# Eight more adaLN modulation units on VectorE: a quad in the first MLP's last group, another from the end of the GLA scan

## The reference, cut to what matters

```python
def adaln(cond, w, b):
    m = jax.nn.silu(cond) @ w + b            # (1 or 2 rows, 2048) @ (2048, 12288), once a layer
    m = m.reshape(cond.shape[0], 6, 1, D_MODEL)
    return [m[:, j] for j in range(6)]

hp = modulate(xp, norm_g[l, 0], sh1p, sc1p)  # rmsnorm(x, g) * (1 + scale) + shift
...
xp = xp + g1p * rmsnorm(yp, norm_g[l, 1])
mp = sq_relu_mlp(modulate(xp, norm_g[l, 2], sh2p, sc2p), w1_mlp[l], w2_mlp[l])
xp = xp + g2p * rmsnorm(mp, norm_g[l, 3])
```

## Time and profile before

| | |
|---|---|
| median of 3 runs | 2492.58 us (2488.64 to 2493.11) |
| the profiled execution | 2489.31 us, of which the span is 2487.5 us |
| granted clock over the span | 0.996 |
| TensorE busy | 2434.9 us (98%) |
| VectorE busy | 1685.1 us (68%) |
| ScalarE busy | 1087.3 us (44%) |
| POOL busy | 262.6 us (11%) |
| read and written in HBM | 634.39 MB and 15.43 MB |

### The profile page before, as it was taken

How to read it: one execution, slowest core, us unless ns; L and a number is a source line. 1 busy time by engine, 2 the same in 40 slices (tenths; PEclk the granted TensorE clock), 3 DMA queues, 4 the chain that set the end, 5 groups by cost and what they waited for, 6 DMA issues and landing times.

```text
span 2487.5 us, 37359 instructions
## 1 busy us (share of the span) xinstructions
PE 2434.9 (98%) x13794; PEld 1991.1 (80%) x13794; DVE 1685.1 (68%) x2118; ACT 1087.3 (44%) x1495; POOL 262.6 (11%) x465
## 2 busy tenths in 40 slices
PE   6899999999999999999999999999999999999998
PEld 3578888778888888888887877798888888888887
DVE  2246665587767767775568877675888678564665
ACT  3234443464333433333454456585644344343343
POOL 0021111000010010000012144200001001000000
PEclk8999999999999999999999999999999999999999
DMA  9999999969888988987877956659668668666564
GB/s 359 372 289 342 321 322 302 320 225 309 294 278 287 308 284 267 310 281 257 281 251 244 307 171 221 222 190 299 204 226 278 208 220 279 197 200 206 169 207 166
DMA packets 458056, 651.39 MB, mean 262 GB/s; under 512 B 21976, under 2 KB 316696, under 8 KB 456280
## 3 DMA queue, kind: packets, MB, share of 16 engines
q1 hardware_dynamic: 426272, 543.47, 65.6%
q0 software_dynamic: 29312, 105.12, 12.6%
q10 hardware_dynamic: 2360, 1.32, 0.2%
HBM read 634.39 MB, written 15.43 MB: 261 GB/s over the span
## 4 chain that ended last, share of the span: by engine, by line
PE 92%; DMA 3%; DVE 2%; ACT 1%; issue 1%; SPq 0%; DVEq 0%; ACTq 0%
PE PS L1380 24%; PE PS L1461 14%; PE PS L1462 14%; PE PS L1463 14%; PE PS L1383 12%; PE PS L1409 3%; DMA SCR<-in_w_ada 1%; DMA RAW<-in_w_o_na 1%; PE PS L1599 1%; PE PS L1391 1%; PE PS L1393 1%; PE PS L1392 1%; PE PS L1600 1%; PE PS L1601 1%; PE PS L1574 1%
## 5 line engine op out<-in xcount | busy, mean ns | idle before, releaser
L2002 DVE TENSOR_TENSOR WLO<-RAW,WHI 128x1024 fp32r<-128x1024 f32 x740 | 873.6, 1225 | 293.0 <-ACT WHI L1715 242.1
L1380 PE MATMUL PS<-HM,WHI 128*128 128x512 f32 x2560 | 648.4, 395 | 3.0 <-issue 2.6
L1715 ACT ACTIVATE WHI<-RAW 128x1024 fp32r<-128x1024 f32 x370 | 390.2, 1055 | 417.0 <-DMA RAW<-in_w_mlp 163.7
L1380 PEld LDWEIGHTS PS<-HM,WHI 128*128 128x128 f32 x2560 | 459.6, 189 | 101.8 <-issue 15.7
L1461 PE MATMUL PS<-WHI,HID 128*128 128x512 f32 x1152 | 450.5, 391 | 0.0
L1462 PE MATMUL PS<-WLO,HID 128*128 128x512 f32 x1152 | 448.4, 389 | 0.0
L1463 PE MATMUL PS<-WHI,HID 128*128 128x512 f32 x1152 | 448.2, 389 | 0.0
L1719 ACT ACTIVATE WHI<-RAW 128x1024 fp32r<-128x1024 f32 x370 | 388.7, 1051 | 97.4 <-DMA RAW<-in_w_mlp 65.4
L1383 PEld LDWEIGHTS PS<-HM,WLO 128*128 128x128 f32 x2560 | 348.9, 190 | 25.6
L1383 PE MATMUL PS<-HM,WLO 128*128 128x256 f32 x2560 | 356.5, 282 | 0.0
L2075 DVE SCALAR_TENSOR_TENSOR X<-X,CS 128x1024 f32<-128x1024 f32 x240 | 297.0, 1279 | 1.4 <-DMA X<-in_w_ada 0.4
(11 more groups left out here) (260 smaller groups left out, 1994.9 us busy)
## 6 DMA issues: line engine op xcount, KB each, us to landing
RAW<-in_w_mlp SPq DMA_DIRECT2D x512, 512.0 KB, 5.4
ADW<-in_w_ada SPq DMA_DIRECT2D x114, 1024.0 KB, 9.9
X<-in_w_ada POOLq DMA_DIRECT2D x224, 256.0 KB, 3.9
RAW<-in_w_qkv_na SPq DMA_DIRECT2D x68, 512.0 KB, 8.6
RAW<-in_w_qkvg_gla SPq DMA_DIRECT2D x64, 512.0 KB, 5.5
SCR<-in_w_ada SPq DMA_DIRECT2D x16, 1024.0 KB, 11.5
RAW<-in_w_o_na SPq DMA_DIRECT2D x32, 512.0 KB, 7.2
RAW<-in_w_qkvg_gla SPq DMA_DIRECT2D x64, 256.0 KB, 5.0
```

Of the source, the lines that this page charges most:

```text
L1380: return mm(bank[:, 0:2 * T2], hi[:, k, P * b:P * b + P], act[:, kc, 0:2 * T2], start=first, stop=False)
L1715: actv(WHI[:, 2 * s + u, 0:HALF], RAW[:, u, 0:HALF], ACT.Copy).then_inc(hi_half, 1)
L2002: tt(WLO[:, 2 * s + u, part], RAW[:, u, part], WHI[:, 2 * s + u, part].bitcast(f32), ALU.subtract).then_inc(done, 1)
```

## The change

Each group of the first MLP now makes four modulation units on TensorE (PU = NB), one in every second up slab, and none in its down slabs (`PLAN_MLP` is empty). The last group of that MLP gets a quad (QV - 1): a tile in each of its eight up slabs, a ninth after the last (`LAST_UP` = 9), four in down slab 0 and three in slab 1 (`LAST_TILES`). TensorE sums it at the end of slab 1 instead of slab 3. POOL puts the first half of `load_gain(1)` ahead of this quad's last tile, and brings X back after it. Another quad, QG, runs from the scan's end: its tiles 0 to 6 in gate slabs r = 19 to 23 (`GATES_FROM`), ahead of `out_lo` in the last, then three, four and two in WO1's slabs 0, 1 and 2 (`GATE_TILES`). TensorE sums it after unit x = 2 of slab 2; ScalarE stores it in slab 2 ahead of the next slab's split, and makes the squares of x parts 0 and 1 after that split instead of in slabs 1 and 2; POOL loads half of the gain ahead of its last two tiles and brings X back only then. The third flush needs the quad of group 2, and the fifth needs QG. GHEAD is loaded without waiting for the scan's quad.

```diff
@@ -182,22 +182,23 @@
...
 A_MLP0 = 5 * D // UC + 1 - SKIP0
-PU = NB + 2
+PU = NB
 GU = PU + QU
-QUADS0, QUADS1 = HID_GROUPS - 1, 2
+QUADS0, QUADS1 = HID_GROUPS, 2
 SKIP = SKIP0 + QUADS0 * QU
-SKIP_V = SKIP + 2 * QU
+SKIP_V = SKIP + 3 * QU
...
 QS = QV + 1
-FROM1 = QS + 1
+QG = QS + 1
+FROM1 = QG + 1
...
 QUAD_UNITS = [A_WO0] + [A_MLP0 + SKIP0 + GU * g + PU for g in range(QUADS0)]
-QUAD_UNITS += [A_WO1 + SKIP, A_WO1 + SKIP + QU, A_MLP1 + SKIP_V, A_END - QU]
+QUAD_UNITS += [A_WO1 + SKIP + QU * q for q in range(3)] + [A_MLP1 + SKIP_V, A_END - QU]
@@ -267,15 +270,15 @@
...
 PLAN_WO0, PLAN_WO, PLAN_V = ((0,), (1,), (), ()), ((0,), (1,), (), ()), ((), (), (), ())
-PLAN_MLP = ((0,), (1,), (), ())
+PLAN_MLP = ((), (), (), ())
...
 mod_rows = nc.dram_tensor("mod_rows", [2 * ADA // UC, 2, 2, 4, P], f32, kind="Internal").ap()
-FLUSHES = [(A_QKV0, 32, A_WO0, 0), (32, 40, 40 - SKIP0, FROM0), (40, 64, 64 - SKIP0 - 2 * QU, FROM0 + 2),
-           (64, 80, A_WO1, QS), (80, 88, 88 - SKIP_V, FROM1), (88, A_END, A_MLP1, FROM1 + QUADS1)]
+FLUSHES = [(A_QKV0, 32, A_WO0, 0), (32, 40, 40 - SKIP0, FROM0), (40, 64, A_MLP0 + 3 * PU, FROM0 + 3),
+           (64, 80, A_WO1, QS + 1), (80, 88, 88 - SKIP_V, FROM1), (88, A_END, A_MLP1, FROM1 + QUADS1)]
@@ -292,6 +295,10 @@
...
 UP_TILES = KC - sum(OUT_TILES)
+GATES_FROM = {3: 1, 4: 1, 5: 1, 6: 2, 7: 2}
+LAST_TILES, GATE_TILES = (4, 3, 0, 0), (3, 4, 2, 0)
+LAST_UP = KC - sum(LAST_TILES)
+assert LAST_UP == 2 * NB + 1
@@ -1073,6 +1080,8 @@
...
             multiply(g)
+        for x in range(GATES_FROM.get(r - R_G, 0)):
+            gate_tile(sum(GATES_FROM.get(q, 0) for q in range(r - R_G)) + x)
@@ -1098,6 +1107,7 @@
...
     pool.wait_ge(hid_done, HID_GROUPS * KC + 2)
+    pool.wait_ge(quad_out, QV * (16 * QU) + 16)
@@ -1153,10 +1163,12 @@
...
             load_states(i + 1)
-    return_x(FROM1)
...
     pool.dma_start(GHEAD, g_head_gla[0:1, :].partition_broadcast(P)).then_inc(sem("ghead_in"), 16)
+    set_picks(4, PICKS)
+    for k in range(KC - 2):
+        quad_load(QG, k)
@@ -1649,7 +1661,10 @@
...
             planned_ada(None if a is None else g * PU + (a + NB), PLAN_MLP)(n, x)
-            if quads is not None and n == YN - 1 and x == 3:
+            if quads is not None and norm is None and n == YN - 1 and x == 3:
+                quad_rows(g + quads, 2 * layer + 2)
+            if quads is not None and norm is not None and n == 1 and x == 3:
+                pe.wait_ge(mod_done, 3)
@@ -1657,8 +1672,9 @@
...
-    mlp(0, M_MLP0, A_MLP0, 2, 0, QUADS0, FROM0)
-    mlp_group(HID_GROUPS - 1, 0, M_MLP0, A_MLP0, 2, 1)
+    mlp(0, M_MLP0, A_MLP0, 2, 0, HID_GROUPS - 1, FROM0)
+    mlp_group(HID_GROUPS - 1, 0, M_MLP0, A_MLP0, 2, 1, FROM0)
+    pe.wait_ge(quad_row, QV + 1)
@@ -1680,6 +1696,8 @@
...
             planned_ada(A_WO1, PLAN_WO)(n, x)
+        if n == 2 and x == 2:
+            quad_rows(QG, 4, QUAD0_BANK)
@@ -1814,6 +1832,10 @@
...
             quad_store(0, QUAD_UNITS[0], QUAD0_BANK)
+        if n == YN - 2 and f == 2:
+            quad_store(QG, QUAD_UNITS[QG], QUAD0_BANK)
+        if n == YN - 2 and f == 1:
+            quad_store(QV - 1, QUAD_UNITS[QV - 1])
@@ -1822,8 +1844,10 @@
...
             store_row(a, at)
-        if 0 < n < YN - 1:
+        if 0 < n < YN - 1 and f not in (1, 2):
             more_squares(f, (("x0",), ("x1",))[n - 1])
+        if n == YN - 2 and f in (1, 2):
+            more_squares(f, ("x0", "x1"))
@@ -2075,10 +2099,15 @@
...
+    def out_tiles(q):
+        if isinstance(q, int) and q in (QV - 1, QG):
+            return GATE_TILES if q == QG else LAST_TILES
+        return OUT_TILES
+
...
         if q is not None:
-            k = UP_TILES + sum(OUT_TILES[:n]) + x
+            k = KC - sum(out_tiles(q)[n:]) + x
@@ -2102,11 +2134,14 @@
...
         split_lo(m + 1, 1)
-        quad_out_tile(quad, n, 0)
+        if quad is not None and out_tiles(quad)[n]:
+            quad_out_tile(quad, n, 0)
+            if n == 2 and f == 2:
+                quad_out_tile(quad, n, 1)
...
             store_gain(f)
-        if flush is not None:
+        if flush is not None and n < YN - 1:
@@ -2115,13 +2150,16 @@
...
                 for x in range(3):
+                    if x == 1 and flush is not None:
+                        sum_rows(flush)
...
         split_lo(m + 2, 0)
-        for x in range(1, OUT_TILES[n]):
-            quad_out_tile(quad, n, x)
+        if quad is not None:
+            for x in range(1 if n < 2 or f != 2 else 2, out_tiles(quad)[n]):
+                quad_out_tile(quad, n, x)
@@ -2316,17 +2354,22 @@
...
         mlp_group(0, layer, m, False, first, False)
-        with dve.Fori(1, quads) as g:
+        with dve.Fori(1, min(quads, HID_GROUPS - 1)) as g:
...
                 mlp_group(g, layer, m)
-        mlp_group(HID_GROUPS - 1, layer, m, True)
+        mlp_group(HID_GROUPS - 1, layer, m, True, HID_GROUPS - 1 + first if quads == HID_GROUPS else None)
...
                 hidden_body(g, i, layer, m)
+        elif complete:
+            hidden_body(g, 0, layer, m, quad, (0, 1), 1)
+            with dve.Fori(1, NB) as i:
+                hidden_body(g, i, layer, m, quad, (0, 1), 1)
+            quad_tile(quad, LAST_UP - 1, (LAST_UP - 1) % 2, NB)
@@ -2336,14 +2379,14 @@
...
-    def hidden_body(g, i, layer, m, quad=None, tiles=()):
+    def hidden_body(g, i, layer, m, quad=None, tiles=(), ahead=0):
...
             if s in tiles:
-                quad_tile(quad, i * 2 + (s - 1), 1 - s, i + (s - 1))
+                quad_tile(quad, i * 2 + (s - 1 + ahead), (1 + s + ahead) % 2, i + ((s + 1 + ahead) // 2 - 1))
@@ -2409,12 +2452,13 @@
...
-    def load_gain(f):
-        pool.wait_ge(gain_row, f + 1)
-        pool.dma_start(gain_rows[f].rearrange("b (k n) -> k b n", k=KC), GAIN_ROW).then_inc(gain_stored, 16)
-        pool.wait_ge(gain_stored, 16 * (f + 1))
+    def load_gain(f, parts=range(YN)):
+        if 0 in parts:
+            pool.wait_ge(gain_row, f + 1)
+            pool.dma_start(gain_rows[f].rearrange("b (k n) -> k b n", k=KC), GAIN_ROW).then_inc(gain_stored, 16)
+            pool.wait_ge(gain_stored, 16 * (f + 1))
         m0 = (M_WO0, output_base(M_MLP0), M_WO1, output_base(M_MLP1))[f]
-        for n in range(YN):
+        for n in parts:
@@ -2471,21 +2516,27 @@
...
         for k in range(KC):
+            if q == QV - 1 and k == KC - 1:
+                load_gain(1, (0, 1))
...
     return_x(QV)
-    load_gain(1)
+    load_gain(1, (2, 3))
...
-    gla_pool(pool, value_quad, quad_load, return_x)
+    gla_pool(pool, value_quad, quad_load, set_picks)
...
         pool.wait_ge(gla_final_out[b], 16 * 2 * GLA_H)
-    load_gain(2)
-    park_x(3, 6)
+    load_gain(2, (0, 1))
+    for k in range(KC - 2, KC):
+        quad_load(QG, k)
+    return_x(FROM1)
+    load_gain(2, (2, 3))
+    park_x(3, 6, None)
```

More of the change, by code:

```diff
@@ L233, in build_program @@
             parts = ("y0", "x0", "y1", "x1", "y2", "x2", "g0", "g1", "x3", "g2")
+            if f in (1, 2):
+                parts = ("y0", "y1", "x0", "x1", "y2", "x2", "g0", "g1", "x3", "g2")
             SQUARES += [(x, f, int(n), b) for x, n in parts for b in range(2) if x == "y" or f < 3]
@@ L939, in build_program, with gla_vector @@
         SILU = {R_G + 3: (0, 1), R_G + 4: (2, 3), R_G + 5: (4,), R_G + 6: (5,), R_G + 7: (6,)}
-        def gla_vector(dve, link, split_lo, evacuate, value_tile, scan_tile):
+        def gla_vector(dve, link, split_lo, evacuate, value_tile, scan_tile, gate_tile):
             ts, tt, stt = nc.vector.tensor_scalar, nc.vector.tensor_tensor, nc.vector.scalar_tensor_tensor
@@ L1089, in gla_vector, with gla_pool @@
             out_lo(3)
-        def gla_pool(pool, value_quad, quad_load, return_x):
+        def gla_pool(pool, value_quad, quad_load, set_picks):
             tt = nc.gpsimd.tensor_tensor
@@ L1267, in with_between @@
                 at = YN - 1 if plan[YN - 2] else YN - 2
-                return plan[n] + ((max(map(max, filter(None, plan))) + 1,) if n == at else ())
+                return plan[n] + ((sum(map(len, plan)),) if n == at else ())
             for n in range(YN):
@@ L1273, in mlp_group, with unit_ada @@
             def mlp_group(g, layer, m, a, at, more=False):
-                def unit_ada(i, x, halves=range(2)):
+                def unit_ada(i, x, halves=range(2), skip=SKIP0):
                     if a is not None:
-                        load_ada(g * PU + i + (a + x), at, g * (GU * UC) + i * UC + ((a + x + SKIP0) * UC - at * ADA), halves)
+                        load_ada(g * PU + i + (a + x), at, g * (GU * UC) + i * UC + ((a + x + skip) * UC - at * ADA), halves)
                 with sp.Fori(0, NB) as i:
@@ L1288, in ada @@
                         if plan:
-                            unit_ada(0, NB + plan[0], halves)
+                            unit_ada(0, NB + plan[0], halves, SKIP0 if NB + plan[0] < PU else SKIP0 + QU)
                     load_out(g * (4 * NB) + (m + 2 * NB), n, w2_mlp[layer], g * D, ada)
@@ L1945, in mlp @@
```

(11 more changed lines are left out.)

## The result

The changed kernel takes **2521.29 us** (median of 4 runs, 2521.01 to 2524.59) against 2492.66 of the kernel before in the same comparison. The ratio is **1.0121, interval [1.0106, 1.0137]**: slower, by 28.6 us between the medians, where +9.2 was forecast. The sign of the likeliest case is right; the time lies 11 us above the upper end of the range. The profiled execution takes 2521.2 us with a span of 2519.2.

What follows compares the result with a forecast made beforehand. TensorE, busy 98% of the span, was taken to bound the kernel. Terms -16.6 removed, +2.2 added, +10.5 (a), +7.9 (b), +5.2 (c) sum to +9.2 on 2492.6: 2501.8 us, range 2481 to 2510.

Steps and rivals of the forecast that it cites:

- the likeliest case: Whole kernel: the change makes it slower, 2498 to 2506 us; chance 43%.
- Removed and added on TensorE: First MLP's groups lose eight units of 2.08 us, -16.6 us; two more quads' rows add 2.2 us.
- The tiles in the up slabs: Group 3, eight up slabs: VectorE has time to spare, so counted at nothing; at most 2.4 us late per slab.
- (a): Group 3, down slabs 0 and 1: gain's turn 4.5 us late, quad's last tile 6 late; +10.5 us, 0.5 to 15.
- tile 15's landing: Group 3, the quad's last load: lands 3.9 us after issue, or 6.8 behind the gain's spreads.
- X comes back ... while slab 2's splits still wait for slots: nothing: Group 3, slab 2: X returns 8.8 us after the quad's rows and costs nothing.
- moving 16 MB from one queue to the other leaves the traffic as it is: First MLP: loads go by POOL's queue instead of SP's, traffic staying 288 GB/s in such a group.
- (b): Gate slabs: seven tiles on VectorE delay the third output turn 6.7 us and the fourth 1.2; +7.9 us, 2.4 to 14.5.
- (c): WO1, slabs 2 and 3: ScalarE's squares wait for X ahead of a split; +5.2 us, nothing to 8.
- The clock: TensorE's clock throughout: the sum leaves it at full, so waits cost nothing beyond themselves.
- the second rival: TensorE's clock falls after three waits of 4 to 7 us, 2.3 us each, 7 more, 2509 us; chance 12%.

Runs made afterwards that it cites:

- e1: Against the changed kernel, group 3's quad is made whole in the up slabs, its last tile's load issued ahead of the gain's store; 13.3 us shorter.
- e2: Against the changed kernel, POOL issues the load of group 3's tile 15 ahead of the gain's store and spreads; 7 us come back.
- e4: Against the changed kernel, the scan-end quad's units return to TensorE and group 3's quad is made in up slabs; 0.18% faster than the kernel before.
- e8: On top of e4, the sum of group 3's quad moves from down slab 1 to down slab 0; 2484.7 us, 0.9976 of the kernel before.
- e6: Against the changed kernel, the tiles in every gate slab stand behind the low parts and the evacuation; 6.4 us won.
- e9: Against the changed kernel, POOL in WO1 issues the loads of tiles 14 and 15 ahead of the gain's store and spreads; 2521.48 us.
- e11: Against the changed kernel, only 16 of X's 2048 columns come back in WO1; 3.6 us shorter by the medians.
- e7: Against the changed kernel, the four squares of x in WO1 stand behind the last units' splits, in slab 3; 2523.0 us.
- e10: The changed kernel's eight units with the edits of e1, e8, e6 and e9 together; 2497.5 us, the kernel before still 0.2% faster.

## Why the prediction was right and wrong, step by step

*Removed and added on TensorE.* Right: 186.0 us a group, 2.08 a unit. The tiles in the up slabs, counted at nothing, are nearly that (e1: 0.86 us).

*(a), 10.5 us; 17.7 measured.* The mechanism is the one named: the gain's turn waits (3.88, predicted 4.5), the quad's rows wait behind tile 15's load behind the gain (9.51, predicted 6). **The term that was mis-sized is tile 15's landing**: "lands 3.9 us later, or 6.8 behind the spreads"; it took 11.0. Some of those 7 us were given back: the gain's store took 3.7 us to the next issue where 5.1 were counted, and TensorE, at half clock behind the turn, came later itself. The median of 224 loads was taken for a load that has four spreads ahead of it and the weights of the down slabs beside it. e2 shows that the order decides it. The upper bound of 15 held for the waits (13.4) and not for the whole, because the clock's 4.3 us lay outside.

*"X comes back ... while slab 2's splits still wait for slots: nothing."* Wrong, as e1, e4 and e8 show: 3 to 4 us in slab 3, hidden in the change itself by the longer waits ahead. The premise that failed with it is "moving 16 MB from one queue to the other leaves the traffic as it is". Over the kernel it does; but group 3 now has a quad, X's return and the weights, and there the bytes have a place.

*(b), 7.9 us; 8.50 of wait and 2.2 of clock.* Right in place and mechanism. The third turn waits 8.50 where 6.7 were forecast, and the fourth, given 1.2, has no wait of its own. e6 shows what the working had missed: two thirds of the wait were avoidable by standing behind the evacuation that ScalarE waits for.

*(c), 5.2 us.* **The step whose mechanism failed.** It gave one wait, by ScalarE's order (squares ahead of a split). The runs show two others in its place: 5.22 us for tiles 14 and 15, whose loads are issued behind the gain's spreads (e9 took this wait to 1.43, but only 2.5 us off the sum of the waits), and 7.67 for weights that land 11 us after their issue, beside X's 2 MB (e11). The squares are worth nothing that the stretch shows (e7). 13.4 us of waits (with one of 0.54 ahead of them) where 5.2 were forecast. The trace before could have told it: X takes 8.8 us in the earlier trace rows, and the units of slab 3 were to load in just those microseconds.

*The clock.* **The largest term that was left out.** The forecast left it at full and gave 12% to the second rival, which puts 7 us on three waits. It happened: 10.2 us on five waits. The rival's price of 2.3 us a wait was near (2.0 measured); its chance and its number of waits were not. The earlier trace rows already held the row that decides, 1.78 us busy in 4 and then 0.50; the row that I leaned on, 8.44 busy in 10 at 1.00, has pauses of 1.2 us. Between them no wait of 4 us stood. Each of those went to half clock here, while a pause of 1.43 (e9) or 1.47 us (e10) before the quad's rows did not: they took 1.07 us. The Trainium skill, "TensorE: Matmul & The Clock Gate", section "What's actually happening", holds that the slow state is the default and that activity releases it. The trace agrees for these five waits (granted clock 0.63 in 1670 to 1680).

*The sum again.* 9.2 forecast, 3.5 more in the waits of (a) and (b) (13.4 + 8.5 against 10.5 + 7.9), 8.2 more in those of (c), 0.8 for the last evacuation, 10.2 of clock: 31.9. The profiled executions' spans differ by 31.7. The medians differ by 28.6; the profiled execution of the kernel before lies 3.3 us under its median.

## What to carry to other kernels

Work given to an engine with idle time is free only where nothing that the full engine needs stands behind it in the same in-order stream; the same seven tiles cost 6 us less behind an evacuation than ahead of it. A transfer's median time says nothing about one that is issued with two megabytes beside it: for each step that is moved, ask what the DMA engines have to do in those very microseconds. And a wait of 4 us or more on TensorE cost some 2 us beyond itself here (10.2 us for five), so each one goes into a sum with that on top.
